# Latent attention layer: key latent first, norms at the evacuations, head lengths in few partitions, queries in two halves

## What is computed

```python
def _mla_mixer(h, w_in, q_a_norm, w_uq, kv_a_norm, w_ukv, q_norm, k_norm, w_out):
    c = h @ w_in
    c_q = c[..., :MLA_Q_LORA]
    c_kv = c[..., MLA_Q_LORA:MLA_Q_LORA + MLA_KV_LORA]
    k_rope = c[..., MLA_Q_LORA + MLA_KV_LORA:]
    q = (_rms_norm(c_q, q_a_norm) @ w_uq).reshape(B, T, MLA_HEADS, MLA_NOPE + MLA_ROPE)
    kv = (_rms_norm(c_kv, kv_a_norm) @ w_ukv).reshape(B, T, MLA_HEADS, MLA_NOPE + MLA_V)
    k = jnp.concatenate([kv[..., :MLA_NOPE], k_rope], axis=-1)
    v = kv[..., MLA_NOPE:]
    q = _rms_norm(q, q_norm)
    k = _rms_norm(k, k_norm)
    ...
    return _dense_attention_blocks(q, k, v) @ w_out
```

## Time and profile before

| what | value |
|---|---|
| three executions | 3635.76, 3626.14, 3631.4 us, median 3631.4 |
| profiled execution | 3632.14 us, span of the trace 3629.2 us |
| PE busy | 3498.6 us, 96% of the span |
| DVE, ACT busy | 2472.0 us (68%), 1521.3 us (42%) |
| chain that ended last | PE 86%, DVE 7%, ACT 3% |

### The profile page before, as it was taken

One profiled execution on the slowest core, in us unless ns is written; L12 is line 12 of the kernel. 1 busy time (PEld: TensorE's weight loads), 2 busy tenths in 40 slices (PEclk: granted clock), 3 DMA queues, 4 the chain that ended last, 5 costly groups with the idle time before them and its releaser, 6 DMA issues.

```text
span 3629.2 us, 66212 instructions
## 1 busy us (share of the span) xinstructions
PE 3498.6 (96%) x27769; PEld 3373.8 (93%) x27769; DVE 2472.0 (68%) x2726; ACT 1521.3 (42%) x1510; POOL 189.8 (5%) x148
## 2 busy tenths in 40 slices
PE   8999999998899997799999999999999999999999
PEld 8998899997799997499999989999998999999899
DVE  7668667664766667666766866666777666677766
ACT  4354334342534343443435433433544343354433
POOL 0000011000000000000000000000241000024100
PEclk9999999999999998799999999999999999998999
DMA  6543374543254543035555325455434545543354
GB/s 249 178 177 121 114 222 176 192 176 133 78 195 166 194 170 131 35 140 187 183 185 178 124 94 188 171 195 187 174 129 151 190 168 197 185 174 128 141 196 162
DMA packets 98920, 593.00 MB, mean 163 GB/s; under 512 B 25684, under 2 KB 26836, under 8 KB 27736
## 3 DMA queue, kind: packets, MB, share of 16 engines
q1 hardware_dynamic: 97280, 586.71, 45.5%
q10 hardware_dynamic: 1496, 4.20, 0.3%
HBM read 588.77 MB, written 2.11 MB: 163 GB/s over the span
## 4 chain that ended last, share of the span: by engine, by line
PE 86%; DVE 7%; ACT 3%; issue 2%; DMA 1%; SPq 0%; DVEq 0%; ACTq 0%
PE prod L423 20%; PE prod L424 20%; PE prod L425 20%; PE acc L425 7%; PE acc L423 7%; PE acc L424 7%; DVE low L1458 2%; ACT high L1047 2%; DVE work L1732 1%; PE acc L610 1%; PE acc L914 1%; PE stat L764 0%; DMA work<-start 0%; PE stat L621 0%; PE acc L681 0%
## 5 line engine op out<-in xcount | busy, mean ns | idle before, releaser
L423 PE MATMUL prod<-xh,high 128*128 128x256 f32 x5840 | 1666.1, 285 | 31.1 <-DVE low L1473 13.0
L424 PE MATMUL prod<-xl,high 128*128 128x256 f32 x5840 | 1652.5, 283 | 0.0
L425 PE MATMUL prod<-xh,low 128*128 128x256 f32 x5840 | 1651.8, 283 | 0.0
L1458 DVE TENSOR_TENSOR low<-raw,high 128x2048 fp32r<-128x2048 f32 x537 | 1239.7, 2309 | 560.5 <-ACT high L1047 554.8
L1047 ACT ACTIVATE high<-raw 128x2048 fp32r<-128x2048 f32 x550 | 1049.0, 1910 | 1033.1 <-PE prod L425 575.9
L423 PEld LDWEIGHTS prod<-xh,high 128*128 128x128 f32 x5840 | 1109.0, 190 | 51.0 <-issue 27.5
L424 PEld LDWEIGHTS prod<-xl,high 128*128 128x128 f32 x5840 | 1109.0, 190 | 0.7
L425 PEld LDWEIGHTS prod<-xh,low 128*128 128x128 f32 x5840 | 1108.6, 190 | 0.0
L425 PE MATMUL acc<-ends,low 128*128 128x256 f32 x2112 | 594.8, 282 | 0.0
L423 PE MATMUL acc<-ends,high 128*128 128x256 f32 x2112 | 594.7, 282 | 0.0
L424 PE MATMUL acc<-ends,high 128*128 128x256 f32 x2112 | 594.6, 282 | 0.0
(11 more groups left out here) (215 smaller groups left out, 2844.8 us busy)
## 6 DMA issues: line engine op xcount, KB each, us to landing
raw<-stream SPq DMA_DIRECT2D x550, 1024.0 KB, 4.8
work<-rpb SPq DMA_DIRECT2D x16, 256.0 KB, 6.4
work<-bias_shifted ACTq DMA_DIRECT2D x2, 1024.0 KB, 5.0
cst<-consts SPq DMA_DIRECT2D x1, 1416.0 KB, 12.3
x<-x_in SPq DMA_DIRECT2D x1, 1024.0 KB, 5.2
raw<-stream SPq DMA_DIRECT2D x2, 512.0 KB, 7.2
work<-bias_by_distance ACTq DMA_DIRECT2D x2, 512.0 KB, 4.5
bias_shifted<-work ACTq DMA_DIRECT2D x1, 1024.0 KB, 6.1
```

Of the source, the lines that this page charges most:

```text
L423: nc.tensor.matmul(out, wh, ah, start=start, stop=False, **kw)
L424: nc.tensor.matmul(out, wh, al, start=False, stop=False, **kw)
L425: return nc.tensor.matmul(out, wl, ah, start=False, stop=stop, **kw)
L1458: v.tensor_tensor(low[:, s % LOW, :], raw[:, s % RAW, :], high[:, s % HIGH, :].bitcast(F32), ALU.subtract).then_inc(low_ready, 1)
```

## The change

It rewrites the latent attention stage. The key latent's slab comes first (the weight stream is permuted on the host). Each latent is split into high and low parts right at its evacuation, with its gain but without its norm: ACT writes the high part to `oh` (a copy with a scale, behind its square of the same pair), DVE the low part to `ol` (`latent_lows`). The norm of the latent is a factor per token, so it is applied later: when DVE empties the bank of a projection it multiplies by `ml_rkv` or `ml_rq` (`evacuated`), and the values, which have tokens in the partitions, by two columns made with two tiny matmuls. The lengths of the heads are summed into 8 rows (16 heads: two groups of 8 rows, 32 partitions apart) by matmuls with 32 output columns, the root is taken of these rows alone, and `spread` (8-row matmuls with a 0/1 matrix, as the neighbourhood attention of layer 2 has them) copies the roots back to all partitions in PSUM, from where DVE multiplies. The queries come in two halves, rope slab first: s+7, s+8, s+9 for heads 0 to 7 and s+10, s+11, s+12 for heads 8 to 15. The roots of the second half's queries are spread between the second and third score steps. The wait of `attention` for the emptied `prod` banks moves from its start to its third step, in the neighbourhood attention as well. Four constant matrices go and one of 36 columns comes: the constants shrink from 2832 to 2100 columns (1416 to 1050 KB).

Its core, with the new main sequences of PE and DVE:

```diff
-        [("ident", P), ("ones", P), ("blk64", P), ("heads", 38), ("whole", 38), ("spread", 4 * P), ("r2n", 2 * P), ("n2r", 2 * P), ("blk32", P), ("rot", P)]
+        [("ident", P), ("ones", P), ("heads", 38), ("whole", 38), ("ropes", 36), ("spread", 4 * P), ("rot", P)]
...
+                for at, out in chunks_out:
+                    a, _ = CONSTS["spread"]
+                    rows = slice(32 * g, 32 * g + 8)
+                    last = nc.tensor.matmul(out, cst[rows, a + 2 * P * at:a + 2 * P * (at + 1):2], guess[rows, q, 0:T], start=True, stop=True)
+                last.then_inc(spread_done, 1)
...
+                def key_sums():
+
+                    q, b = n_stat[0] % 2, stat_bank()
+                    pe.wait_ge(sq_ready, c.up(sq_ready, 5))
+                    for g in range(2):
+                        for at in range(4):
+                            nc.tensor.matmul(b[32 * g:32 * g + 32, 0, :], con("heads", 6 - 2 * at, 32), ml_sqn[:, 4 * g + at, :],
+                                             start=(at == 0), stop=False)
+                        last = nc.tensor.matmul(b[32 * g:32 * g + 32, 0, :], ones[0:ROPE, 0:32], ml_sqk[0:ROPE, :], start=False, stop=True)
+                def query_sums(half):
+
+                    q, b = n_stat[0] % 2, stat_bank()
+                    pe.wait_ge(sq_ready, c.up(sq_ready, 3))
+                    for at in range(2):
+                        nc.tensor.matmul(b[0:32, 0, :], con("ropes", 4 - 4 * at, 32), ml_sqr[:, 2 * half + at, :], start=(at == 0), stop=False)
+                    for at in range(4):
+                        last = nc.tensor.matmul(b[0:32, 0, :], con("heads", 6 - 2 * at, 32), ml_sqn[:, 4 * half + at, :], start=False, stop=(at == 3))
                     last.then_inc(stat_done, 1)
+
+                opening(s, False)
+                project(s + 2)
+                pe.wait_ge(sq_ready, c.up(sq_ready))
+                stats([(ones, ml_sq[:, 6 + i, :]) for i in range(2)])
+                project(s + 3)
+                project(s + 4, n_chunks=1)
+                pe.wait_ge(sq_ready, c.up(sq_ready, 3))
+                stats([(ones, ml_sq[:, i, :]) for i in range(MLA_Q // P)])
+                pe.wait_ge(norm_ready, norms + 1)
+                b = stat_bank()
+                for tt in range(TT):
+                    last = nc.tensor.matmul(b[:, 0, tt:tt + 1], ml_rkv[0:1, tt * P:(tt + 1) * P], ones[0:1, 0:1], start=True, stop=True)
+                last.then_inc(stat_done, 1)
+                pe.wait_ge(mix_ready, mixes + 2)
+                keys_and_values(s + 5)
+                rotate(9, [ml_kr[:, 0, :]])
+                keys_and_values(s + 6)
+                up(s + 7)
+                qk = key_sums()
+                up(s + 8)
+                rotate(10, [ml_qg[:, i, :] for i in range(2)])
+                pe.wait_ge(root_ready, c.up(root_ready))
                 for j in range(4):
+                    spread(qk, [(2 * j + i, acc[j][:, i, :]) for i in range(2)])
+                up(s + 9)
+                for g in range(2):
+                    pe.wait_ge(norm_ready, norms + 1 + g + 1)
+                    spread_ropes(qk, g, [(i, acc[g][:, i, :]) for i in range(2)])
+                q0 = query_sums(0)
+                up(s + 10)
+                up(s + 11)
+                rotate(11, [ml_qg[:, 2 + i, :] for i in range(2)])
+                pe.wait_ge(root_ready, c.up(root_ready))
+                b = bank()
+                roped = n_prod[0]
+                spread_ropes(q0, 0, [(i, b[:, i, :]) for i in range(2)])
+                    spread(q0, [(2 * j + i, acc[2 + j][:, i, :]) for i in range(2)])
+                up(s + 12)
+                q1 = query_sums(1)
+                pe.wait_ge(norm_ready, norms + 1 + 4 + 2 + 2)
+                pe.wait_ge(evac, roped)
...
+                step(0)
+                step(1)
+                pe.wait_ge(root_ready, c.up(root_ready))
+                b = bank()
+                spread_ropes(q1, 0, [(i, b[:, i, :]) for i in range(2)])
+                for j in range(2):
+                    b = bank()
+                    spread(q1, [(2 * j + i, b[:, i, :]) for i in range(2)])
+                pe.wait_ge(var_ready, n_stat[0])
+                for i in range(2, MLA_HEADS // 2 + 3):
+                    step(i)
...
+                def evacuated(out, bank, row):
+                    own(v.tensor_tensor(out, bank[:, :, :], over(row, 2), ALU.mult), evac)
...
+                token_norm(s)
+                scaled(pair(ml_c, 3), product(s)[:, :, :])
+                lows(s)
+                scaled(pair(ml_c, 0), product(s + 1)[:, :, :])
+                latent_lows(6, 7)
+                lows(s + 1)
+                scaled(pair(ml_c, 1), product(s + 2)[:, :, :])
+                latent_lows(0, 1)
+                lows(s + 2)
+                q = variance(T, MLA_KV)
+                scaled(pair(ml_c, 2), product(s + 3)[:, :, :])
+                latent_lows(2, 3)
+                inverse_root(q, T, ml_rkv, norm_ready)
+                lows(s + 3)
+                latent_lows(4, 5)
+                own(v.tensor_tensor(ml_krr, product(s + 4)[:, 0, :], rstd[:, :], ALU.mult), evac)
+                own(v.tensor_scalar(ml_kr[:, 0, :], ml_krr, par("mla_kr"), None, ALU.mult), mix_ready)
+                lows(s + 4)
+                q = variance(T, MLA_Q)
+                columns()
+                inverse_root(q, T, ml_rq)
                 for j in range(2):
-                    own(v.tensor_copy(ml_qr[:, 2 * j:2 * j + 2, :], product(s + 11 + j)[:, :, :]), evac)
-                    lows(s + 11 + j)
-                dve.wait_ge(sq_ready, c.up(sq_ready, 6))
-                for j in range(2):
-                    v.tensor_scalar(ml_qr[:, 2 * j:2 * j + 2, :], ml_qr[:, 2 * j:2 * j + 2, :], par("mla_qr"), None, ALU.mult).then_inc(mix_ready, 1)
-                dve.wait_ge(mix_ready, c.up(mix_ready, 2))
-                for j in range(2):
-                    rotation(ml_qr[:, 2 * j:2 * j + 2, :], ml_qr[:, 2 * j:2 * j + 2, :], 2)
-
-                for r in range(4):
-                    last = lengths(False, r)
-                    own(last, norm_ready if r == 3 else vec_step)
-                attention(MLA_HEADS, "mla")
+                    for u in range(2):
+                        m = 2 * j + u
+                        evacuated(pair(ml_kn, m), product(), ml_rkv)
+                        values_of(m)
+                    lows(s + 5 + j)
+                    if j == 0:
+                        rotation(ml_kr[:, 0:1, :], act3(4)[:, 5:6, :], 1)
+                evacuated(pair(ml_qr, 0), product(s + 7), ml_rq)
+                gained(0)
+                lows(s + 7)
+                k = variance(T, NOPE + ROPE, rows=64)
+                evacuated(pair(ml_qn, 0), product(s + 8), ml_rq)
+                inverse_root(k, T, signal=root_ready, rows=64)
+                lows(s + 8)
+                dve.wait_ge(sq_ready, c.up(sq_ready, 1 + 3 + 1 + 4 + 1))
+                rotation(pair(ml_qg, 0), pair(ml_qr, 0), 2)
+                for m in range(4):
+                    normed(pair(ml_kn, m), "mla_kn", acc[m])
+                evacuated(pair(ml_qn, 1), product(s + 9), ml_rq)
+                lows(s + 9)
+                for g in range(2):
+                    dve.wait_ge(spread_done, c.up(spread_done))
+                    v.tensor_tensor(pair(ml_kr, g), over(ml_krot, 2), acc[g][:, :, :], ALU.mult).then_inc(norm_ready, 1)
+                    c.up(norm_ready)
+                q = variance(T, NOPE + ROPE, float(NOPE + ROPE), rows=32)
+                evacuated(pair(ml_qr, 1), product(s + 10), ml_rq)
+                gained(1)
+                inverse_root(q, T, signal=root_ready, rows=32)
+                lows(s + 10)
+                evacuated(pair(ml_qn, 2), product(s + 11), ml_rq)
+                lows(s + 11)
+                dve.wait_ge(sq_ready, c.up(sq_ready, 3))
+                rotation(pair(ml_qg, 1), pair(ml_qr, 1), 2)
+                b = prod[n_prod[0] % 2]
+                n_prod[0] += 1
+                normed(pair(ml_qr, 0), None, b, evac)
+                for m in range(2):
+                    normed(pair(ml_qn, m), "mla_qn", acc[2 + m])
+                evacuated(pair(ml_qn, 3), product(s + 12), ml_rq)
+                lows(s + 12)
+                q = variance(T, NOPE + ROPE, float(NOPE + ROPE), rows=32)
+                c.up(sq_ready, 2)
+                step = attention(MLA_HEADS, "mla")
+                step(0)
+                inverse_root(q, T, signal=root_ready, rows=32)
+                step(1)
+                for j in range(3):
+                    b = prod[n_prod[0] % 2]
```

More of the change, by code:

```diff
@@ L597, in attention, with step @@
                 pairs = heads // 2
-                pe.wait_ge(evac, n_prod[0])
                 exps = c.now(exp_done)
                 c.up(exp_done, heads)
-                for i in range(pairs + 3):
+                def step(i):
+                    if i == 2:
```

(64 more changed lines are left out.)

184 lines of the change are left out of this document (77 added, 107 removed).

## The result

| | before | after |
|---|---|---|
| median of the runs on one chip | 3628.8 us (3622.7 to 3635.8) | 3563.9 us (3558.9 to 3568.0) |
| ratio, 95% interval | | 0.9824 [0.9805, 0.9843] |
| span of the profiled execution | 3629.2 us | 3560.0 us |

The account below looks back on a forecast made before the run. PE was taken as the bound, losing time to waits for DVE and the lower clock. Work 83.3, waits 16.5 and clock 17.9 make 117.7 us in place of 152.2; with smaller constants, 3596 us, range 3577 to 3614.

Parts of the forecast that it names:

- two banks in lockstep: First keys to slab s+12: PE stands for each of 17 banks, 59.5 us of waits, ending slower at 3655; chance 0.04.
- no change: Whole kernel: the weight stream or a queue behind it takes over, time 3630; chance 0.03.
- the clock stay down in the query slabs: Slabs s+7 to s+12 run at 0.50 throughout, adding 20 us for 3616; chance 0.12.
- The clock that stays up: Latent stage: short waits never lower the clock and scores run at 1.00, giving 3580; chance 0.15.
- The clock term: Latent stage up to the first transposes: 17.9 us lost to the lower clock, in place of 22.9.
- the 83.3 of the sum: Latent stage: PE's own work after the change at the full clock, 83.3 us, 5.6 less than before.
- The three pairs of scores ran at 0.50 throughout before. I take that over: Scores ending the stage: half clock again after a 2.4 us wait, losing 3 x 2.04 = 6.1 us, plus 0.7 for a spread.
- The seven episodes ahead of the scores: Four waits and three spreads before the scores each lower the clock, together losing 11.1 us.
- my one row of 1443 us: Profile before: PE worked 0.51 of two us from 1441, then clock 0.50; taken to show that two-us waits lower it.
- I measure the stage from 1362.57 us: Slab s+2's start to first transposes at 1514.74, 152.2 us before; both programs taken as the same outside.
- a change in another layer of more than 2 us: Layers outside the latent stage: a change above 2 us there would show the forecast wrong.
- the forecast's 35.4 us: Whole kernel's predicted gain: 34.5 us in the latent stage and 0.9 from smaller constants.

Follow-up runs that it names:

- the run with the later root: The kernel after, with the query latent's root refined on DVE behind the emptying of the first keys and values instead of ahead: 3562.6 us, 0.9816.
- the run with the old places: The kernel after, with an unused 728-column tensor and root buffers at their old size, so every tensor stands where it stood before: 3591.6 us, 0.9898.

## Why the prediction was off

**The mechanism of the stage was right.** Counted from the start of slab s+2 (the first scores of the forecast are worked back from its sum):

| | forecast | measured |
|---|---|---|
| keys start | 18.0 us | 18.2 |
| wait before the second keys | 3.9 | 3.5 |
| before the values (bank of the rotated key) | 2.3 | 2.0 |
| before the keys' spread | 1.3 | 1.3 |
| before the queries' first sums | 0.9 | 1.6 |
| before the first queries' spread, the last sums | 2.4, 2.4 | 2.7, 2.7 |
| third spread, third scores | 2.3, 0.8 | 1.4, 0.9 |
| all waits | 16.5 | 16.8 |
| first scores | 97.8 | 98.3 |
| first transposes | 117.7 | 114.0 |

From the transposes to the next block it is 64.8 us before and 64.7 after, as said. Start-up gave 0.95 us (the first token sums come at 21.39 in place of 22.34), where I took 0.9. That agreement is worth little: in the other runs these sums come at 21.05 to 22.21 us with the new constants and at 23.77 in the one with the old. The rivals of two banks in lockstep and of no change did not come about (the longest wait is 3.5 us), nor did the clock stay down in the query slabs. The clock that stays up came about in part.

**The clock term was too large.** 17.9 us were to be lost. The clock was low for 23.5 us between 1349.83 and 1463.82, PE idle for 0.9 of them, so 11.3 us were lost. PE's own work is then 114.0 - 16.8 - 11.3 = 85.9 us, 2.6 more than the 83.3 of the sum; where these 2.6 us lie stays open. The term had two parts. "The three pairs of scores ran at 0.50 throughout before. I take that over", with the spread between them, was to lose 6.8 us and lost 2.8: two of the three ran at 1.00, behind a wait of 2.67 us. The seven episodes ahead of the scores were to lose 11.1 us and lost 8.5, since only four came: 3.4 us each behind the waits of 3.5 and 2.0 us and the keys' spread, and 6.8 us behind the first queries' spread with its wait.

```profile
1445.00:1448.00 3.00, 2.52 (x12) 1.23 (x12) 2.24 (x1) 0.34 (x1) 0.00 (x0) 1.00 0.02 5
1448.00:1453.00 5.00, 5.00 (x34) 2.40 (x32) 2.55 (x6) 2.31 (x9) 0.00 (x0) 1.00 0.57 210
...
1459.00:1464.00 5.00, 4.79 (x17) 2.22 (x18) 0.19 (x2) 0.00 (x0) 0.00 (x0) 0.50 0.00 0
```

(Stretches of the kernel after: PE, PEld, DVE, ACT and POOL busy, then PEclk, DMA share, GB/s.) The same wait can go either way. With every activation at its old place, the wait of 2.67 us ahead of the last sums is there again, and the clock is at 0.50 behind it:

```profile
1459.46 1.02 PE L879 MATMUL stat<-work,cst 128*32 128x256 f32 x4 [2.67 <-ACT work L1121]
```

```profile
1461.00:1464.00 3.00, 3.00 (x8) 1.22 (x8) 0.64 (x2) 0.00 (x0) 0.00 (x0) 0.50 0.42 147
```

It is low there in five of the eleven profiles with this wait ahead of the scores, and at 1.00 in six. So a wait of this length lowers the clock in one execution and not in another of the same code, and my one row of 1443 us could not price each. The rule that I had weighed, in the Trainium skill, "TensorE: Matmul & The Clock Gate", section "Loop structure matters more than you think", is that emptying PSUM by DVE leaves the array warm. The trace disagrees with it behind the wait of 2.03 us for such an emptying (0.50 from 1386 to 1389) and agrees in the run with the later root (1.00 behind 2.37 us). I had called all waits ones of this sort; the two ahead of the queries' sums are for a square on ACT, so the rule does not bear on them. With every activation at its old place and waits the same to 0.1 us, the stage's piece had 41.0 us of low clock against 27.3, and took 190.5 us against 184.1.

**The step that failed** is the one that was never a term: "I measure the stage from 1362.57 us [...] up to which both programs do the same" and "behind which both attentions are again the same". I priced everything outside the stage at nothing because its instructions are the same. Their operands had moved, and what I had put at nothing measured 31 us. Against the run with the old places, the kernel after is 27.7 us faster by the medians and 32.4 us shorter in span: 20.7 us in the twelve feed-forward blocks (16.3 in the ten pieces above, 3.1 in the first block, 1.4 in the last), 6.4 us in the piece with the stage, 5.1 us net in the other mixers (3.9 in the first, 2.6 in the last, and 1.6 us longer in the fourth layer's), and 0.1 at the start. That the places make the pitch is shown; how the 11.5 us in the mixers divide between pitch and clock is not. An estimate: over the six mixers the clock was low for 145.2 us with the old places and 141.5 in the kernel after, at half rate 1.8 us at most, so most of it would be pitch. My own sign of error, "a change in another layer of more than 2 us", was met.

For the same code at the old places the forecast's 35.4 us stand against 34.4 measured, and part of that agreement is luck. The stage took 116.5 us, 1.2 less than the 117.7 of the sum. But from the transposes to the next block it took 68.6 us there, 3.8 more than before, with the clock low for 11.5 us of it in place of 3.1. The piece with the stage thus gave 31.8 us in span; the other mixers, whose code is the same but for one moved wait in the neighbourhood attention, gave 3.8 net and the start 0.8. Of the twelve profiles with the changed stage, six have 64.4 to 65.4 us for that stretch, the kernel after among them, and six 68.3 or 68.6: "the time from there to the output projection stays as it is" held only in half of them.

## What to carry to other kernels

Where PE is the bound and its matmuls run back to back, count them in a stretch before and after: a change of a buffer's size far from the work moved the pitch of the feed-forward blocks by 0.8% here, and other places moved it by up to 4.5%. An edit can be credited with, or robbed of, some 20 to 50 us that it didn't earn. Test an edit with the streamed operands held at their old addresses, and try some places of the activations by themselves, since 32 bytes were worth 23 us in either kernel. Waits between engines can be walked from written order and row durations to some tenths of a us; what the clock makes of them can't, and needs a range of its own.

## What the runs showed of the hardware

- The mean pitch of 128x256 matmuls at the full clock changed with the place in SBUF of the activations: 113.3, 116.7, 117.3, 117.8, 118.7 and 120.0 ns were seen, and each lasts a whole block. Which buffer it hangs on, the mechanism, and why blocks of one program differ stay open.
- The same wait of the same code lowered the clock in one execution and not in another: 2.67 us on ACT was followed by 1.00 in the kernel after and by 0.50 with the old places. At another point 2.03 us on DVE was followed by 0.50, and in the run with the later root 2.37 us by 1.00.
- Behind the wait of 2.67 us, 64-row fp32 scores ran at 1.00 for two pairs (5.12 us); behind a wait of 2.9 us and three 8-row spreads they ran at 0.50 for three (13.91 us).
